# Retention moved into the gate chunks of the input projection: a two-layer streaming encoder step on one core

## The reference, cut to what matters

```
def retention_layer(x, c, pos, r0, norm_g, ada_w, ada_b, w_in, gn_g, w_out):
    shift, scale, gate = jnp.split(ada_mod(c, ada_w, ada_b), 3, axis=-1)
    h = modulate(x, norm_g, shift, scale)
    q, k, v, g = jnp.split(h @ w_in, [RET_QK_W, 2 * RET_QK_W, 2 * RET_QK_W + RET_VW], axis=-1)
    q, k = rotary(q, pos), rotary(k, pos) * (RET_DK ** -0.5)
    o, r = retention_scan(q, k, v, r0)          # per head: o = (q k^T * decay) v + q r * decay;  r = r * decay + k^T v
    o = head_norm(o, gn_g) * jax.nn.silu(g)
    return x + gate[:, None, :] * (o @ w_out), r
```

## Time and profile before

| | |
|---|---|
| time, median of 3 runs | 1979.88 us (1979.63 to 1983.1) |
| the profiled execution | 1980.21 us, of it 1978.6 us span |
| TensorE matmuls busy | 1807.5 us, 91% |
| VectorE, ScalarE, GpSimd busy | 775.8, 520.0, 421.0 us |
| mean granted clock of TensorE | 0.964 |
| DMA | 269.87 MB, mean 136 GB/s |

### The profile page before, as it was taken

How to read it: one execution, slowest core, us unless ns; L and a number is a source line. 1 busy time by engine, 2 the same in 40 slices (tenths; PEclk the granted TensorE clock), 3 DMA queues, 4 the chain that set the end, 5 groups by cost and what they waited for, 6 DMA issues and landing times. The chain is left out here.

```text
span 1978.6 us, 25290 instructions
## 1 busy us (share of the span) xinstructions
PE 1807.5 (91%) x8585; PEld 1375.8 (70%) x8585; DVE 775.8 (39%) x1358; ACT 520.0 (26%) x939; POOL 421.0 (21%) x600
## 2 busy tenths in 40 slices
PE   3799999999999959989969899999999788998698
PEld 0799987777678744434448788888888656766576
DVE  1664440001100115767633334645540055665242
ACT  3311111111111111111111224334221146666220
POOL 1311110000100004334412125324010103323121
PEclk8899999999999989999989999999999969999899
DMA  8253333333333335986574212312222152232442
GB/s 311 72 179 134 124 130 131 131 127 127 120 120 128 130 112 220 346 306 250 202 282 131 96 43 96 112 54 86 90 91 91 55 151 63 73 113 69 125 160 75
DMA packets 144164, 269.87 MB, mean 136 GB/s; under 512 B 18517, under 2 KB 64497, under 8 KB 142802
## 3 DMA queue, kind: packets, MB, share of 16 engines
q1 hardware_dynamic: 111618, 182.00, 27.2%
q0 software_dynamic: 22416, 67.83, 9.2%
q10 hardware_dynamic: 10048, 18.94, 2.5%
HBM read 181.60 MB, written 87.11 MB: 136 GB/s over the span
## 5 line engine op out<-in xcount | busy, mean ns | idle before, releaser
L1129 PE MATMUL mid_ps_o<-w_hi,mid_hT_lo 128*128 128x512 f32 x720 | 287.9, 400 | 0.0
L1129 PE MATMUL mid_ps_o<-w_hi,mid_hT_hi 128*128 128x512 f32 x720 | 286.7, 398 | 0.8 <-DVE mid_hT_lo L1253 0.8
L1129 PE MATMUL mid_ps_o<-w_lo,mid_hT_hi 128*128 128x512 f32 x720 | 284.8, 396 | 0.0
L218 DVE TENSOR_TENSOR w_lo<-w_raw,w_hi 128x1024 fp32r<-128x1024 f32 x80 | 97.7, 1223 | 435.9 <-ACT w_hi L206 428.8
L707 PE MATMUL in_ps_o<-w_hi,in_hT_hi 128*128 128x512 f32 x576 | 228.9, 397 | 0.0
L707 PE MATMUL in_ps_o<-w_hi,in_hT_lo 128*128 128x512 f32 x576 | 228.4, 396 | 0.0
L707 PE MATMUL in_ps_o<-w_lo,in_hT_hi 128*128 128x512 f32 x576 | 226.4, 393 | 0.0
L1129 PEld LDWEIGHTS mid_ps_o<-w_lo,mid_hT_hi 128*128 128x128 f32 x720 | 136.0, 189 | 33.6
L1129 PEld LDWEIGHTS mid_ps_o<-w_hi,mid_hT_hi 128*128 128x128 f32 x720 | 136.0, 189 | 31.9 <-issue 1.1
L1129 PEld LDWEIGHTS mid_ps_o<-w_hi,mid_hT_lo 128*128 128x128 f32 x720 | 135.7, 189 | 31.6
L651 ACT ACTIVATE x<-in_ps_o 128x512 f32<-128x512 f32 x72 | 43.1, 598 | 353.1 <-PE in_ps_o L707 353.1
(11 more groups left out here) (249 smaller groups left out, 2792.9 us busy)
## 6 DMA issues: line engine op xcount, KB each, us to landing
w_raw<-in_a_w_in SPq DMA_DIRECT2D x96, 256.0 KB, 3.0
ret_r_in<-in_state_ret SPq DMA_DIRECT2D x32, 512.0 KB, 7.3
out_state_sample<-ret_r_in ACTq DMA_DIRECT2D x32, 512.0 KB, 13.6
scratch_qkT<-x POOLq DMA_DIRECT2D x48, 192.0 KB, 2.3
scratch_v<-x POOLq DMA_DIRECT2D x36, 256.0 KB, 2.6
scratch_g<-x POOLq DMA_DIRECT2D x36, 256.0 KB, 2.6
ret_g<-scratch_g SPq DMA_DIRECT2D x4, 2304.0 KB, 18.1
scratch_o<-ret_ost POOLq DMA_DIRECT2D x36, 256.0 KB, 4.5
```

The source lines that it names most:

```text
L218: dve.tensor_tensor(pr.w_lo[:, slot, sub * KS:(sub + 1) * KS, :], pr.raw[:, sub % 2], pr.w_hi[:, slot, sub * KS:(sub + 1) * KS, :].bitcast ...
L1129: ins = pe.matmul(ps_o[:, n % 4, :], h[:, k, t * P:(t + 1) * P], w[:, slot, k, :], start=k + m == 0, stop=k == KT - 1 and m == 2)
```

## The change

`project("in")` is replaced by `intake`, which has only the eight chunks of q/k and v; its twelve slots of the other modulations are spread over these (`slots`), and their ends follow in chunks 4 to 6 (`end_at`). The normalized, transposed input stays in SBUF (`hT_hi`, `hT_lo`, now allocated for the whole stretch), and all other buffers share one area (`room`).

`retention` and `middle` are replaced by `trunk`, one stage with fourteen chunks: the four gate chunks, one for each head, and the ten as before. In a gate chunk each tile's 24 product matmuls are followed by that tile's retention. The gate stays on chip: ScalarE evaluates SiLU from PSUM, and GpSimd multiplies it with the scaled output. Decay factors sit in a table of seven columns for each head (`cols`) and one causal mask, and factors that depend on the query row drop out in the head norm, so q is no longer scaled on GpSimd; decay powers of the state are immediates.

The eight stream states are worked in four strips for each head (`strips`, at tiles 2, 4, 6 and 8), of 4 streams x 128 key rows each. A strip has four matmuls with 32 output columns as before, and four updates that each use only 32 rows of the array, those of the stream pair, in four row groups, each into its own PSUM bank (`STRIP`); VectorE then updates four 128x512 parts. GpSimd issues the stores of the states, ScalarE did before; SP loads the next strip into the buffer once its store has landed.

In the last head, TensorE also transposes the first half of the o rows (`half_turn`: heads 0 and 1), tile by tile over the place in `hT` that the tile's gate product has read, so that the first residual chunk follows without a stage boundary. Row loads for the second half are issued one for each tile. The boundary between gate product parts 0 to 4 and 5 to 7 of a tile is where strips stand.

```diff
+    slots = [(0, 8), (1, 3), (1, 9), (2, 3), (2, 9), (3, 3), (3, 9), (4, 2), (4, 6), (5, 2), (5, 6), (6, 3)]
...
+    end_at = {(4, 4): 0, (5, 0): 1, (6, 6): 2}
...
+        PS_S, PS_O, PS_U, PS_STR, PS_T = 2, 3, 4, 6, 7
+        STRIP = [(3, PS_S), (0, PS_U), (1, PS_U + 1), (2, PS_T)]
...
+            def load_r(k):
+
+                h, q = divmod(k, 4)
+                par, a = q // 2, q % 2
+                if k >= 2:
+                    sp.wait_ge(r_stored[k % 2], 64 * (k // 2))
+                for j in range(4):
+                    sp.dma_start(r[:, k % 2, j], dr["state_ret"][2 * j + par, h, a * P:(a + 1) * P, :]).then_inc(r_in[k % 2], 16)
...
+                            orow_load(t + 1, half)
+                    if t == 1:
+                        load_weights(h + 1, 2)
+                        load_qk(3 * h + 2)
+                    if t < PT and 8 * h + t + 3 < RH * PT:
+                        load_v(8 * h + t + 3)
+                    if t == 3:
+                        load_weights(h + 1, 3)
+                    if t in (2, 4, 6, 8) and 4 * h + t // 2 - 1 + 2 < 4 * RH:
+                        load_r(4 * h + t // 2 - 1 + 2)
+                    if t == 5:
+                        load_weights(h + 2, 0)
+                        if h + 1 < RH:
+                            load_qk(3 * h + 3)
+                    if t == 7:
+                        load_weights(h + 2, 1)
+                        if h + 1 < RH:
+                            load_qk(3 * h + 4)
+                    if t == 8 and h + 1 < RH:
+                        load_vs(h + 1)
+                    if t == 8 and h == RH - 2:
+                        for half in range(2):
+                            sp.wait_ge(o_stored[half], 16 * T)
+                            orow_load(0, half)
...
+            def update(h, c):
+
+                n = 8 * h + c
+                pe.wait_ge(decayed, score_no(h, c) + 1)
+                pe.wait_ge(v_in[n % 3], 16 * (n // 3 + 1))
+                if n:
+                    pe.wait_ge(state_new, n)
+                for a in range(2):
+                    ins = pe.matmul(ps[:, PS_U + a, :], k_tok[:, c % 2, a * P:(a + 1) * P], v[:, n % 3], start=True, stop=True)
+                ins.then_inc(upd, 1)
...
+            def strips(h, q):
+
+                i = 4 * h + q
+                par, a = q // 2, q % 2
+                pe.wait_ge(r_in[i % 2], 64 * (i // 2 + 1))
+                pe.wait_ge(qs_ready, h + 1)
+                for j in range(4):
+                    ins = pe.matmul(ps[BR * j:BR * (j + 1), PS_STR, :], qs[:, par, a, BR * j:BR * (j + 1)], r[:, i % 2, j, :],
+                                    start=False, stop=q == 3, tile_position=(0, BR * j), skip_group_check=True)
+                ins.then_inc(o_done if q == 3 else s_ready, 1)
+                pe.wait_ge(decayed, score_no(h, min(2 * q + 2, 7)) + 1)
+                pe.wait_ge(state_new, 8 * h + 2 * q + 2)
+                if i:
+                    pe.wait_ge(strip_new, 4 * i)
+                if h == RH - 1:
+                    pe.wait_ge(half_ready, 2 * (2 * q + 2))
+                for j, bank in STRIP:
+                    part = slice(BR * j, BR * (j + 1))
+                    ins = pe.matmul(ps[:, bank, :], k_str[part, par, a * P:(a + 1) * P], vs[part, :], start=True, stop=True, tile_position=(BR * j, 0))
+                ins.then_inc(strips_done, 1)
+
...
+            for h in range(RH):
+                pe.wait_ge(pr.raw_split, SUBS * (C0 + h) + SUBS + 2)
+                for t in range(T):
+                    n = h * T + t
+                    if n >= 2:
+                        pe.wait_ge(g_evac, n - 1)
+                    product(n, range(0, 5))
+                    if t == 0:
+                        if h:
+                            pe.wait_ge(strip_new, 16 * h)
+                        score(h, 0)
+                    if strip_tile(t) is not None:
+                        strips(h, strip_tile(t))
+                    product(n, range(5, KT))
+                    if t + 1 < PT:
+                        if strip_tile(t) is not None:
+                            pe.wait_ge(strip_new, 4 * (4 * h + strip_tile(t)) + 1)
+                        score(h, t + 1)
+                    if h == RH - 1:
+                        half_turn(t, 0)
+                    if t < PT:
+                        if strip_tile(t) is not None:
+                            pe.wait_ge(strip_new, 4 * (4 * h + strip_tile(t)) + 3)
+                        update(h, t)
+                        output(h, t)
+                    if t == 0:
+                        score(h, SELF)
+                    if t == 1:
+                        self_output(h)
+                    if h == RH - 1:
+                        half_turn(t, 1)
+            stage_of = [None, None, 0, 0, 1, 1, 2, 2, 2, 2]
+            for j in range(NG, CHUNKS):
...
+            for h in range(RH):
+                for t in range(T):
+                    n = h * T + t
+                    act.wait_ge(out_done, n + 1)
+                    if n:
+                        act.wait_ge(gated, n)
+                    act.activation(g_t[:, :], ps[:, n % 2, :], ACT.Silu).then_inc(g_evac, 1)
+                    if h == RH - 1:
+                        half_high(t, 0)
+                        half_high(t, 1)
+                    act.wait_ge(moments, n + 1)
+                    act.activation(sc[:, 0:1], mv[:, 1:2], ACT.Sqrt, bias=cols[:, h, 5 + int(t == SELF):6 + int(t == SELF)]).then_inc(ret_root, 1)
+                    act.wait_ge(coef, n + 1)
+                    if n >= 2:
+                        act.wait_ge(o_stored[n % 2], 16 * (n // 2))
+                    act.activation(o_t[:, n % 2], ps[:, PS_STR if t == SELF else PS_O, :], ACT.Identity, bias=sc[:, 2:3], scale=sc[:, 1:2]).then_inc(o_scaled, 1)
+                    if t % 2 and t < 2 * SUBS:
+                        split_hi(pr, act, C0 + h + 1, (C0 + h + 1) % 2, t // 2, gain=pr.gn_g[:, 0] if h + 1 == NG else None)
...
+                        pool.wait_ge(strip_new, 4 * i + 4)
+                        for j in range(4):
+                            pool.dma_start(dr["state_sample"][2 * j + par, h, a * P:(a + 1) * P, :], r[:, i % 2, j]).then_inc(r_stored[i % 2], 16)
+                    if t == SELF:
+                        pool.wait_ge(state_new, PT * h + PT)
+                        pool.dma_start(dr["state_prompt"][h].rearrange("(a p) c -> p a c", p=P), state[:, :, :]).then_inc(p_stored, 16)
+                    pool.wait_ge(g_evac, n + 1)
+                    pool.wait_ge(o_scaled, n + 1)
+                    pool.tensor_tensor(o_t[:, n % 2], o_t[:, n % 2], g_t[:, :], ALU.mult).then_inc(gated, 1)
+                    pool.wait_ge(gated, n + 1)
+                    pool.dma_start(dr["o"][t * P:(t + 1) * P, h * DV:(h + 1) * DV], o_t[:, n % 2]).then_inc(o_stored[n % 2], 16)
...
+            def new_strips(h, q):
+
+                i = 4 * h + q
+                dve.wait_ge(strips_done, i + 1)
+                dve.wait_ge(*((o_done, T * h + T) if q == 3 else (s_ready, 3 * h + q + 1)))
+                for j, bank in STRIP:
+                    dve.scalar_tensor_tensor(r[:, i % 2, j], r[:, i % 2, j], GAMMA[h] ** DEC_SEQ, ps[:, bank, :], ALU.mult, ALU.add).then_inc(strip_new, 1)
...
+            for h in range(RH):
+                for t in range(T):
+                    n = h * T + t
+                    if t == 0:
+                        decay(h, 0)
+                    if strip_tile(t) is not None:
+                        new_strips(h, strip_tile(t))
+                    if t + 1 < PT:
+                        decay(h, t + 1)
+                    if h == RH - 1:
+                        half_low(t, 0)
+                    statistics(h, t)
+                    if t < PT:
+                        new_state(h, t)
+                    if t == 0:
+                        decay(h, SELF)
+                    coefficients(n)
+                    if h == RH - 1:
+                        half_low(t, 1)
+                    if t % 2 and t < 2 * SUBS:
+                        split_lo(pr, dve, C0 + h + 1, (C0 + h + 1) % 2, t // 2, gain=pr.gn_g[:, 0] if h + 1 == NG else None)
+            dve.wait_ge(gate_in[0], 16)
...
-        source = ExitStack()
-        x = source.enter_context(nc.sbuf_tensor("x", [P, TILES * D], F32))
-        condition(pr, x, x_rows, qk[0])
-        project(pr, "in", None, True, 0,
-                [dict(kind="rotary", pairs=2, weights=qk, store=turned_rows),
-                 dict(kind="copy", pairs=2, weights=wv, store=to_rows("v")),
-                 dict(kind="silu", pairs=2, weights=wg, store=to_rows("g"))], 0, wo[0][0], rows_here=x, side=True, after_gain=pr.gn_g[:, 0])
-        source.close()
-        retention(pr)
-        middle(pr, x_rows, [wo[0][0], wo[0][1], wo[1][0], wo[1][1], wk, wvv, *wq, *wg2], wo2[0])
+        acts = ExitStack()
+        room = acts.enter_context(nc.sbuf_tensor("room", [P, ROOM], F32))
```

(94 more changed lines are left out.)

1036 lines of the change are left out of this document (606 added, 430 removed).

## The result

The changed kernel takes 1895.6 us (median of 4 runs, 1892.0 to 1897.8) against 1981.5 us of the kernel before in the same comparison: a ratio of 0.9565, 95% interval 0.9549 to 0.9580. The forecast was 1894, its range 1872 to 1936. The profiled execution took 1897.8 us, its span 1896.1.

The account below looks back on a forecast made before the run. TensorE was taken to bound retention (90%) and nearly all the rest. Savings of 8.9 and 16.3 us at the two boundaries, 43.2 in retention and 17.3 in the ten chunks sum to 85.7: 1980.2 becomes 1894 us, range 1872 to 1936.

Parts of the forecast that it names:

- Hole one: TensorE's idle gap between input projection and retention: 24.9 us before, forecast at 11.6 plus 3 for the lowered clock.
- Boundary two: Gap between retention's last update and the first residual product: all 16.3 us go, as residual chunk 0 follows in the stream.
- Row groups, the largest term: State updates of the eight sequences, four at once on 32 rows each: 54.9 us become 14.6, saving 40.3.
- Tiles: Gate tiles of the merged stage: 10.6 us each, 12.5 with strips, with TensorE busy throughout.
- Stalls: Waits looked for in the merged retention, on VectorE, gate evacuation, SP's queue and modulation slots: 9 us allowed.
- Step (c): SP's single queue: state loads wait for stores, other loads queue behind; buffers fit, next head's sample values tight, 2 us.
- The rival of SP's order: State stores landing at 17 us or later delay three head changes or a dozen strip tiles: 21 to 25 us, 1917; chance 0.09.
- the prediction's own signs of being wrong: Gate tiles with TensorE waiting over 1 us for VectorE or DMA; SP late at head changes; clock falling in gate stage.
- VectorE in strip tiles: Strip updates queue behind the odd tile's weight split; the third update lands at 8.1 us, just when TensorE needs it.
- Table loads: 72 ScalarE loads, 92.4 us, forecast off TensorE's path, deciding only from some 6 us more per tile; rival 1987, chance 0.10.
- Ten chunks: The stage behind retention: 17.3 us saved, from transposes leaving 6.1, waits for output rows 7.2 and clock 4.
- boundary one: Between input projection and retention: 24.9 us before, 16.0 after including clock and moved transposes, so 8.9 us saved.

Follow-up runs that it names:

- the three runs on the kernel before: Kernel before with row-group state updates alone, 1982.4 us; also with masks by two operations a head, 1983.9; also with an unused matmul ahead of each step, 1981.0.

## Why the prediction was right

Against its own steps:

- **Boundaries.** Hole one was forecast at 11.6 us and 3 for the clock; it is 12.35 and 2.8. The 1.4 us for the moved transposes did not come. Boundary two went whole. Right.
- **Row groups, the largest term.** 40.3 us were forecast from bounds that lay 40 apart; in place it is 16 x 2.37 = 38 for the strips. The value nearest to the column groups was the right one to take, but no row showed row groups, so that the largest term came out this close is in part luck. What the prediction did not say is that this term hangs on the merge: it priced the row groups as TensorE work that disappears wherever it stands, and the three runs on the kernel before show that there it brings nothing. It had read the retention stretch by its means (TensorE 235 of 260 us, DMA share 0.72), which do not show that at the head changes the load of g is as long as TensorE's work beside it. So "TensorE waited for neither", of the g rows' store and load, was wrong: TensorE's 7.0 us of waits for scaled queries stand behind that load. The merge keeps g on the chip, and it puts products between a strip's updates and what has to wait for VectorE.
- **Tiles.** Forecast 10.6 us for a gate tile, 12.5 with a strip; 10.55 (tiles 3 and 5) and 12.82 (tiles 2, 4 and 6), in the first three heads. Without stalls the four heads come to 193.8 us of retention for 197.7 forecast. The half transposes cost 8.7 for 8.6.
- **Stalls.** 9 us were allowed, 13 came, all in the last head: 10.7 at its first tile, 2.2 at the end, 0.3 between. The size was nearly right and the place was not. Step (c) named the strip's store, the state load that waits for it, and what is queued behind, but only as "the sample values of the next head", at 2 us. That the first o rows stand in the same queue one place further on was overlooked; they, and not the sample values, are needed in the next tile. The rival of SP's order is what happened, at one head change of three and with half its price. Its premise, slower stores at 17 us or more, was wrong: stores land in 5.0 us. It was the wait alone. With this, two of the prediction's own signs of being wrong did appear, once each: SP was late at a head change, and the clock fell inside the gate stage.
- **VectorE in strip tiles.** "No wait, but no margin": there is no wait, and 0.85 us of margin.
- **Table loads.** Off the path, as forecast; the room is at least 3.0 us a tile and less than 8.9, which takes in the 6 that were said.
- **Ten chunks.** 17.3 us of 17.3; no wait for rows, granted clock 1.00. The share of transposes, waits and clock in it was not measured apart.

The stalls cost 4 us more than allowed and the tiles 4 less; attention's stretch took 3.7 more and boundary one 1.0 less. The profiled execution is 3 to 4 us above the forecast, and the median lies 2.2 below the profiled execution. The 1.6 us between forecast and median are better than the steps were; that much is luck.

## What to carry to other kernels

Price an edit where it stands: the same row groups that saved 38 us between products saved nothing in a stage where TensorE then waited for a load that they do not shorten, and ran behind its waits at the lower clock. A mean over a stage (0.72 of the DMA engines) does not show a stretch of 19 us in which they are full: look at the places where the stage changes. Merging two stages that are both bound by one engine can pay, if one has waits that the other's work can fill. When a step moves, list what stands behind each waiting instruction in its queue, to the end of the list and with the time at which each is needed: here one load behind a wait cost 10.8 us, and moving two loads gave it back.

## What the runs showed of the hardware that was not expected

- Less TensorE work between waits came with a lower clock: with the row groups a stretch of 270 us fell from a granted clock of 0.97 to 0.86 and became no shorter; 14 us of matmuls whose result nobody uses, put into the waits, brought it to 0.92 and cost nothing.
- A change of ScalarE's table costs its load of 1.28 us and no more in these traces: the rows of a pair of SiLU and root on one column add up to 2.97 us, 2 x 1.28 for the loads and 2 x 0.20 for the functions, and the next pair starts 3.00 us behind the first. The Trainium skill (ScalarE: Activation LUTs, What ACT_TABLE_LOAD costs) counts about 2.66 us a switch; the trace does not show the second half of that.
- A queue can be late while every transfer is quick: SP stood 8 us on one wait, with a median landing of 4.1 us for state loads and 5.0 for their stores, of 256 KB each.
